# Hybrid mLSTM and attention encoder step: mLSTM heads computed token-major, rotary swap by DVE shuffle, attention heads handled in pairs, on one core

## The reference, cut to what matters

```python
w = jnp.exp(d - m_t[..., None]) * jnp.einsum('bhtd,bhsd->bhts', q, k)
inter = jnp.exp(g - m_t)
num = inter[..., None] * jnp.einsum('bhtd,bhde->bhte', q, C) + jnp.einsum('bhts,bhse->bhte', w, v)
den = inter * jnp.einsum('bhtd,bhd->bht', q, n) + jnp.sum(w, axis=-1)
h = num / jnp.maximum(jnp.abs(den), jnp.exp(-m_t))[..., None]
...
h = h * lax.rsqrt(jnp.mean(h * h, axis=-1, keepdims=True) + EPS)
...
m = jnp.maximum(jnp.max(s, axis=-1, keepdims=True), sk)
p = jnp.exp(s - m)
return p / (jnp.sum(p, axis=-1, keepdims=True) + jnp.exp(sk - m))
```

## Time and profile before

| | us |
|---|---|
| median of 3 runs | 1113.93 (1113.78 to 1116.93) |
| the profiled execution | 1115.43 |
| its span | 1113.6 |
| TensorE busy | 1103.8 (99%) |
| TensorE weight load busy | 1080.8 (97%) |
| DVE busy | 703.9 (63%) |
| ACT busy | 511.2 (46%) |
| POOL busy | 114.1 (10%) |
| mean granted clock, share of full speed | 0.995 |

### The profile page before, as it was taken

The page is one execution under the profiler, slowest core; times in us unless marked ns, Lnnn a source line. Parts: engine busy times, 40 slices in busy tenths (PEclk is TensorE's granted clock), DMA queues, the critical chain, the costliest instruction groups (busy, mean ns, idle before and its releaser), DMA issues.

```text
span 1113.6 us, 21313 instructions
## 1 busy us (share of the span) xinstructions
PE 1103.8 (99%) x8147; PEld 1080.8 (97%) x8147; DVE 703.9 (63%) x1079; ACT 511.2 (46%) x760; POOL 114.1 (10%) x146
## 2 busy tenths in 40 slices
PE   9999999999999999999999999999999999999998
PEld 8999999998999999999999999999988899999998
DVE  7766665474665876665546666655599776666442
ACT  6544443363554544444335444433466554444331
POOL 0000001200002600000210000011142410000011
PEclk9999999999999999999999999999999999999999
DMA  7544454333233644445434445543332244444431
GB/s 274 190 151 173 179 183 178 118 114 109 100 129 111 207 172 167 172 165 206 159 113 168 172 151 173 201 164 142 114 148 92 83 173 160 172 167 179 176 136 43
DMA packets 24493, 172.07 MB, mean 155 GB/s; under 512 B 3280, under 2 KB 3568, under 8 KB 5888
## 3 DMA queue, kind: packets, MB, share of 16 engines
q1 hardware_dynamic: 22320, 167.45, 42.0%
q0 software_dynamic: 960, 2.23, 0.6%
q10 hardware_dynamic: 1168, 1.77, 0.5%
HBM read 168.88 MB, written 2.56 MB: 154 GB/s over the span
## 4 chain that ended last, share of the span: by engine, by line
PE 93%; DVE 4%; ACT 1%; DMA 1%; issue 1%; POOL 0%; SPq 0%; DVEq 0%; ACTq 0%
PE acc L395 30%; PE acc L397 29%; PE acc L396 29%; DVE wlo L382 1%; DMA raw<-in_w 1%; PE num L464 1%; DVE rstd L1042 1%; PE mb L675 0%; PE mb L694 0%; PE mb L609 0%; PE num L601 0%; PE acc L722 0%; ACT work L955 0%; ACT whi L353 0%; PE mb L422 0%
## 5 line engine op out<-in xcount | busy, mean ns | idle before, releaser
L395 PE MATMUL acc<-xhi,whi 128*128 128x288 f32 x1680 | 502.2, 299 | 0.3 <-DVE wlo L382 0.3
L353 ACT ACTIVATE whi<-raw 128x1024 fp32r<-128x1024 f32 (+1 forms) x290 | 326.6, 1128 | 381.2 <-PE acc L397 363.3
L396 PE MATMUL acc<-xlo,whi 128*128 128x288 f32 x1680 | 497.0, 296 | 0.0
L397 PE MATMUL acc<-xhi,wlo 128*128 128x288 f32 x1680 | 495.3, 295 | 0.0
L382 DVE TENSOR_TENSOR wlo<-raw,whi 128x1024 fp32r<-128x1024 f32 (+1 forms) x290 | 384.2, 1326 | 158.0 <-ACT whi L353 147.3
L395 PEld LDWEIGHTS acc<-xhi,whi 128*128 128x128 f32 x1680 | 316.1, 188 | 3.0 <-issue 1.8
L397 PEld LDWEIGHTS acc<-xhi,wlo 128*128 128x128 f32 x1680 | 317.7, 189 | 0.0
L396 PEld LDWEIGHTS acc<-xlo,whi 128*128 128x128 f32 x1680 | 316.8, 189 | 0.5
L395 PE MATMUL acc<-ahi,whi 128*128 128x288 f32 x832 | 247.1, 297 | 0.9 <-DVE alo L1279 0.7
L396 PE MATMUL acc<-alo,whi 128*128 128x288 f32 x832 | 245.4, 295 | 0.0
L397 PE MATMUL acc<-ahi,wlo 128*128 128x288 f32 x832 | 244.6, 294 | 0.0
(11 more groups left out here) (225 smaller groups left out, 642.9 us busy)
## 6 DMA issues: line engine op xcount, KB each, us to landing
raw<-in_w SPq DMA_DIRECT2D x113, 1024.0 KB, 4.8
raw<-in_w SPq DMA_DIRECT2D x32, 1408.0 KB, 5.8
x<-in_xT SPq DMA_DIRECT2D x4, 288.0 KB, 5.3
raw<-in_w SPq DMA_DIRECT2D x4, 256.0 KB, 4.8
out_yT<-x ACTq DMA_DIRECT2D x2, 288.0 KB, 2.2
out_yT<-x SPq DMA_DIRECT2D x2, 288.0 KB, 2.3
work<-in_cst POOLq DMA_DIRECT2D x1, 560.0 KB, 4.2
work<-in_c ACTq DMA_DIRECT2D x1, 514.0 KB
```

The source lines that it names most:

```text
L353: act.activation(dst, src, ACT.Copy).then_inc(hi_done, 1)
L395: pe.matmul(out, wh, hi[:, k, :], start=(first and n == 0), stop=False)
L396: pe.matmul(out, wh, lo[:, k, :], start=False, stop=False)
L397: mm = pe.matmul(out, wl, hi[:, k, :], start=False, stop=(last and n == len(tiles) - 1))
```

## The change

**mLSTM.** The heads' output is now made with tokens on partitions (token-major): for the three token tiles `M_TOK` (0, 128, 160; the last one overlaps, and its last 32 rows are the sample), five matmuls of 257 columns with the weights `wts` as the stationary operand give numerator and denominator together (`vtok` and `c0` have the ones column and the normaliser as 257th). The sum of squares is then ACT's `accum_out`, and denominator, root and scale are columns of 128 x 3, all three tiles at once. DVE scales the heads (`hs`), TensorE transposes them back (6 transposes, step 2), and step 2 also gates them. Steps are four instead of five, at pieces 8, 12, 17 and 22. The gate weights' hi and lo lie side by side in one tile `gw`, so that 16 matmuls do what 24 did. The rows of decays are no longer spread by matmuls: SP writes them to DRAM (`bounce`) and loads them back over all partitions (`through_memory`), behind the load of the stage's sixth unit; six transposes of 4 rows (`row_turn`) give the columns.

**Attention.** Features of a head are laid out so that the swap stays within 32 partitions; DVE's `stream_shuffle` does it, and the ten matmuls of L722 go. POOL multiplies the swapped tile by the sine, DVE the other by the cosine. The items become *pairs*: DVE and ACT do maximum, negation, exps and division of both heads together; one of the pair's scalings goes to ACT (`scaled`). The pair's scores follow a piece (even tick), the values are put into the middle of the next piece (odd tick), and each tick transposes one head. Pieces 4 to 11 carry the pairs 0 to 7. In the tail, more of the partial output products stand between the ticks. The 36 matmuls at the program's end (`long`), whose result nothing reads, are removed.

The core of the diff:

```diff
-SWA_PIECES = ["k0", "q0", "v0", "q1", "q2", "q3", "k1", "q4", "q5", "q6", "v1", "q7"]
+SWA_PIECES = ["k0", "q0", "q1", "v0", "q2", "q3", "k1", "q4", "q5", "q6", "v1", "q7"]
...
+PAIRS = [("p", 0), ("p", 1), ("p", 2), ("p", 3), ("s", 0), ("p", 4), ("p", 5), ("p", 6), ("s", 1), ("p", 7)]
+NP = len(PAIRS)
+PAIR_AT = {4 + n: n for n in range(8)}
+TAIL_TICKS = range(2 * len(PAIR_AT) - 1, 2 * NP + 5)
+
+
+FILL = {16: [(0, [0, 1]), (0, [2, 3]), (1, [0, 1])], 17: [(1, [2, 3])], 18: [(2, [0, 1])],
+        19: [(2, [2, 3]), (3, [0, 1])], 21: [(3, [2, 3])], 23: [(0, [4, 5, 6])], 24: [(m, [4, 5, 6]) for m in (1, 2, 3)]}
+
+HEAD_START = (8, 12, 17, 22)
+HEAD_STEPS = {p + s: (h, s) for h, p in enumerate(HEAD_START) for s in range(4)}
...
+            def through_memory():
+
+                sp.wait_ge(em_ready, 1)
+                sp.dma_start(bounce, r_all).then_inc(bounce_in, 16)
+                sp.wait_ge(bounce_in, 16)
+                every = bounce.rearrange("(a h) n -> a h n", a=1).to_broadcast([P, NH, T + TS])
+                sp.dma_start(spread[:, :, :], every).then_inc(spread_in, 16)
...
+            def row_turn():
+
+                pe.wait_ge(em_ready, 2)
+                for t, at in enumerate(M_TOK):
+                    for q, src in enumerate((r_em, row[0])):
+                        to = (2 * t + q) * NH
+                        mm = pe.transpose(mb[1][:, to:to + NH], src[:, at:at + P], ident[0:NH, 0:NH])
+                mm.then_inc(at_mm, 1)
...
+                    pe.wait_ge(wts_ready, 3 * (h + 1))
+                    N = DV + 1
+                    pe.matmul(mb[0][:, 0:N], wts[:, 0:128], vtok[:, 0, :], start=True, stop=True).then_inc(out_mm, 1)
+                    pe.matmul(mb[1][:, 0:N], wts[:, 128:256], vtok[:, 0, :], start=True, stop=False)
+                    pe.matmul(mb[1][:, 0:N], wts[:, 256:384], vtok[:, 1, :], start=False, stop=True).then_inc(out_mm, 1)
+                    pe.matmul(mb[2][:, 0:N], wts[:, 384:512], vtok[:, 2, :], start=True, stop=False)
+                    pe.matmul(mb[2][:, 0:N], qi[:, :], c0[:, h, :], start=False, stop=True).then_inc(out_mm, 1)
...
-                    pe.wait_ge(den_used, h + 1)
-                    pe.wait_ge(sqs_ready, h + 1)
-                    pe.matmul(mb[2][:, 0:T], ones, sqn[:, 0, :], start=True, stop=True).then_inc(ssq_mm, 1)
+                    pe.wait_ge(hs_ready, 3 * (h + 1))
+                    for t in range(3):
+                        for e in range(2):
+                            mm = pe.transpose(mb[e][:, t * P:(t + 1) * P], hs[:, t, e * P:(e + 1) * P], ident)
+                    mm.then_inc(ht_mm, 1)
...
+            def transposes(n):
+
+                if not 0 <= n < 2 * NP:
+                    return
+                pe.wait_ge(p_ready, n + 1)
+                if PAIRS[n // 2][0] == "p":
+                    pe.wait_ge(p_act, sum(k == "p" for k, _ in PAIRS[:n // 2 + 1]))
+                if n >= 1:
+                    pe.wait_ge(pt_ready, n)
...
+            def values(n, G0):
+
+                if not 0 <= n < NP:
+                    return
+                kind, c = PAIRS[n]
+                pe.wait_ge(pt_ready, 2 * n + 2)
+                pe.wait_ge(evac, G0 + group_of("last", f"v{c // 4 if kind == 'p' else c}") + 1)
+                if n >= 1:
+                    pe.wait_ge(olo_ready, n)
...
+                transposes(t - 3)
+                if t % 2 == 0:
+                    pair_scores(t // 2)
+                else:
+                    values((t - 5) // 2, G0)
...
-                            in_piece(i, 0, c0_ + n, g, G0 + g)
-                    elif what == "swap":
-
-                        pe.wait_ge(evac, max(G0 + group_of("piece", p) + 1, G0 + g - 3))
-                        pe.matmul(bank, perm, s_raw[:, ROPE.index(p) % 2, :], start=True, stop=True).then_inc(turn_mm, 1)
-                    else:
-                        pe.wait_ge(evac, max(G0 + group_of("piece", p) + 1, G0 + g - 3))
-                        for t, (at, m) in enumerate(TOK):
+                            t = 2 * PAIR_AT[n - 1] + 1 if n - 1 in PAIR_AT else None
+                            in_piece(i, 0, c0_ + n, g, G0 + g, between=None if t is None else lambda: tick(t, G0))
+                        if n in PAIR_AT:
+                            tick(2 * PAIR_AT[n], G0)
...
-            long = ahi[:, 0:2, :].rearrange("p a t -> p (a t)")
-            for cols, n in ((P, T), (P, 512), (P, 256), (P, 320), (96, T), (P, P)):
-                for r in range(6):
-                    pe.matmul(acc[2 + r % 2][0:cols, 0:n], whi[:, 0, r, 0:cols], long[:, 0:n], start=True, stop=True)
...
+                    act.activation(warm[:, 7:8], epst[:, :], ACT.Sqrt)
+                    for t in range(3):
+                        act.wait_ge(out_mm, 3 * h + t + 1)
+                        act.activation(hs[:, t, :], mb[t][:, 0:DV], ACT.Square, accum_out=ss[:, t:t + 1]).then_inc(sumsq, 1)
+                    act.wait_ge(y_ready, h + 1)
+                    act.activation(rinv[:, :], dd[:, :], ACT.Sqrt, scale=1.0 / DV).then_inc(sd_ready, 1)
...
+                probs_turned(t - 3)
+                if t % 2 == 0:
+                    scaled(t // 2 - 1)
+                    outputs_hi((t - 6) // 2)
+                    exps(t // 2)
...
+                for n, p in enumerate(SWA_PIECES):
+                    hi_ahead(0, c0_ + n)
+                    if n in PAIR_AT:
+                        if n - 1 in PAIR_AT:
+                            tick(2 * PAIR_AT[n] - 1)
+                        tick(2 * PAIR_AT[n])
...
+                    dve.wait_ge(sumsq, 3 * (h + 1))
+                    den = num[:, :, DV]
+                    own(dve.tensor_copy(dd[:, :], den))
+                    own(dve.tensor_tensor(dd[:, :], dd[:, :], dd[:, :], ALU.mult))
+                    dve.wait_ge(cols_ready, 1)
+                    own(dve.tensor_tensor(dd[:, :], dd[:, :], cols[:, :, 0, h], ALU.max))
+                    dve.scalar_tensor_tensor(dd[:, :], dd[:, :], DV * EPS, ss[:, :], ALU.mult, ALU.add).then_inc(y_ready, 1)
+                    dve.wait_ge(sd_ready, h + 1)
+                    own(dve.reciprocal(rinv[:, :], rinv[:, :]))
+                    for t in range(3):
+                        dve.tensor_scalar(hs[:, t, :], mb[t][:, 0:DV], rinv[:, t:t + 1], None, ALU.mult).then_inc(hs_ready, 1)
...
+                            dve.stream_shuffle(s_sw[:, xi % 2, :], bank, SWAP_16)
+                            dve.tensor_tensor(s_t1[:, xi % 2, :], bank, rc, ALU.mult).then_inc(evac, 1)
+                        if n in PAIR_AT:
+                            scores(PAIR_AT[n])
+                        lo_ahead(0, c0_ + n)
+                        if n in PAIR_AT:
+                            outputs_lo(PAIR_AT[n] - 3)
+                            divide(PAIR_AT[n])
...
```

More of the change, by code:

```diff
@@ new lines, in exps @@
+            def exps(n):
+                if n >= NP:
+                    return
+                b = n % 2
+                parts = ((0, P), (P, 3 * P)) if PAIRS[n][0] == "p" else ((0, CACHE + TS),)
+                act.wait_ge(neg_ready, n + 1)
+                for u in range(2):
+                    for j, (lo_, hi_) in enumerate(parts):
+                        v = prob[:, (2 * n + u) % 4, lo_:hi_]
+                        act.activation(v, v, ACT.Exp, bias=s_neg[:, b, u, j:j + 1], accum_out=s_sum[:, b, u, j:j + 1])
+                act.wait_ge(z_exp, n + 1)
+                J = len(parts)
+                act.activation(s_sk[:, b, :, 0:J], s_z[:, b, :, 0:J], ACT.Exp).then_inc(exp_ready, 1)
@@ new lines, in divide @@
+            def divide(n):
+                if not 0 <= n < NP:
+                    return
+                b = n % 2
+                p = PAIRS[n][0] == "p"
+                parts = ((0, P), (P, 3 * P)) if p else ((0, CACHE + TS),)
+                J = len(parts)
+                dve.wait_ge(exp_ready, n + 1)
+                own(dve.tensor_tensor(s_den[:, b, :, 0:J], s_sum[:, b, :, 0:J], s_sk[:, b, :, 0:J], ALU.add))
+                dve.reciprocal(s_inv[:, b, :, 0:J], s_den[:, b, :, 0:J]).then_inc(inv_ready, 1)
+                dve.wait_ge(inv_ready, n + 1)
+                for u in range(2):
```

651 lines of the change are left out of this document (287 added, 364 removed).

## The result

| | before | after |
|---|---|---|
| median, us | 1115.43 (1113.78 to 1118.40, 4 runs) | 1127.17 (1125.98 to 1129.44, 4 runs) |
| the profiled execution | 1115.43 | 1125.98 |
| its span | 1113.6 | 1124.2 |
| ratio of after to before | | 1.011, 95% interval 1.0093 to 1.0127 |
| TensorE busy | 1103.8 | 1084.5 |

The kernel became 1.1% slower, by 11.7 us, where 5.4 were forecast; 1127.17 lies 0.2 us above the range. TensorE has 19 us less of busy time, and the kernel is slower all the same: the work went and waits came. The medians leave out a single execution, one of the twelve of run 1, which took 1461.53 us at a mean granted clock of 0.675.

What follows compares the result with a forecast made beforehand. TensorE's work was taken as the price, with any new wait added whole. mLSTM -10.4 and attention +15.8 us summed to +5.4: 1120.8 us profiled, 1119.3 us median (0.5% slower), with an 8-in-10 range of 1105 to 1127.

Steps and rivals of the forecast that it cites:

- mLSTM heads, TensorE work: mLSTM stage: rebuilt steps save TensorE 1.9 us for each of four heads, -7.6 us.
- row spreads and their two clock drops: mLSTM: transposes replace the 4-row spreading matmuls, -4.8 us, and two stretches at low clock go, -3.0 us.
- waits for the scaled heads: mLSTM: TensorE waits before step 2, 0.3 us three times and 3.7 us at the last head, together +4.6 us.
- clock behind them: mLSTM: one drop of TensorE's clock after the idle time at the last head, +1.5 us.
- slots of pieces 5 and 6: Attention's first two slots: nothing to transpose at their ends, so 4.6 and 4.8 us.
- slots of pieces 8 to 11: Attention: four slots of 8.84, 7.8, 8.75 and 8.8 us, both waits in the order of queues included.
- tail: From piece 11's end to the end of the partial output products: 30.3 us against 25.50, +4.8 us.
- The two waits in the slots: Attention slots: TensorE idles 1.74 us for ACT's copy behind its split, 1.16 us for DVE's outputs_lo; slot 8.84 us.
- One clock drop after the 3.7: +1.5: Attention, slot of piece 7: TensorE waits 3.7 us for ACT, then one low-clock stretch costs 1.5 us.
- the clock falls in the slots too: Rival: repeated waits in attention slots lower TensorE's clock, six drops of 1.5 us, 1128 us; chance 0.12.
- the slots keep TensorE's pace: Rival: in attention ACT's copy and DVE's outputs_lo come in time, slots take 5.7 us, 1097 us in all; chance 0.16.
- Only the first wait: Rival: DVE's scores and split end 1.2 us sooner, slots and tail 6 us shorter, 1113 us; chance 0.22.

Runs made afterwards that it cites:

- run 1: Changed kernel with ACT's copy of the head transposed in mid-piece put ahead of its split of weights: 1115.36 us, ratio 1.0001 to the kernel before.
- run 2: Changed kernel with DVE's outputs_lo put ahead of its split of weights, behind the scores: 1123.05 us, ratio 1.0069 to the kernel before.
- run 3: Changed kernel with both the edits of run 1 and run 2: 1111.08 us, ratio 0.9955 to the kernel before.
- run 4: Changed kernel with 29 unread products of zeros filling TensorE's wait in the slot of piece 7: 1124.11 us, ratio 1.0075 to the kernel before.
- run 8: Kernel of run 3 with the partial output products behind piece 11 moved and reordered: 1105.81 us, ratio 0.9908 to the kernel before.
- run 9: Changed kernel with the edits of run 3, run 6, run 7 and run 8 together: 1097.48 us, ratio 0.9850 to the kernel before.
- run 5: The mLSTM part of the change alone, attention and its projection as in the kernel before: 1101.96 us, ratio 0.9879 to the kernel before.
- run 7: Kernel of run 3 with ACT's copy of the very first transposed head ahead of the second pair's exps: 1107.21 us, ratio 0.9924 to the kernel before.
- run 6: Changed kernel with the last mLSTM head's step 2 behind two pieces of partial output products: 1121.05 us, ratio 1.0050 to the kernel before.
- run 10: Kernel of run 5 with the last mLSTM head's step 2 behind two pieces of partial products: 1097.76 us, ratio 0.9852 to the kernel before.

## Why the prediction was right and wrong

The direction and the two places in the queues were right; the size was half of what was measured, since the low clock in attention was put at 1.5 us and cost about 5, and the time fell just outside the range. Two errors partly cancelled: mLSTM gave 2.1 us more than forecast, and attention with what follows it cost 7.5 us more. Without the first the miss would have been larger. By the steps of the sum, profiled execution against profiled execution (measured: from the times at which the pieces' last products start, and the waits as the trace has them):

| step | forecast | measured |
|---|---|---|
| mLSTM heads, TensorE work | -7.6 | -8.6 |
| gates | -1.1 | -1.1 |
| row spreads and their two clock drops | -7.8 | -7.8 |
| waits for the scaled heads | +4.6 | +3.3 |
| clock behind them | +1.5 | +1.6 |
| attention to piece 4 | -1.1 | -1.3 |
| slots of pieces 5 and 6 | 4.6 and 4.8 | 5.84 and 4.56 |
| slot of piece 7, clock in it | 9.8 + 1.5 | 12.79 |
| slots of pieces 8 to 11 | 34.2 | 34.75 |
| tail | 30.3 | 32.92 |
| rest of the projection, and the block behind | 0 | +1.6 and +0.4 |

**mLSTM: right.** -12.5 against -10.4. The row spreads, the gates and the trip through memory (no wait, as taken) came out to a tenth of a microsecond. Heads 0 to 2 had none of the 0.3 us waits, and the last waited 3.31 us instead of 3.7. For the matmul of 32 rows the forecast took the price of its row. TensorE: Matmul & The Clock Gate of the Trainium skill (table "Why this matters for your kernels") has a K=32 matmul as long as one of K=128. The traces here speak for the row: with 257 columns one of 32 rows took 0.63 us before, and one of 128 rows 0.43 from start to start after. The heads gave 8.6 us, where the row's price made it 7.6 and the equal price 6.8; no run changed the rows alone.

**The two waits in the slots: right, in place, releaser and length.** Forecast 1.74 and 1.16 us, measured 1.68 and, in the slots of pieces 8 and 10, 1.17 and 1.28 (0.54 and 0.89 in the other two); a slot 8.84, measured 9.00. Runs 1 to 3 take them away one by one.

**The step that failed: the size of the clock drops in attention.** "One clock drop after the 3.7: +1.5" took 3.41 us at the low level from the opening. The wait was there (3.93 us), and 6.82 us at 0.50 came behind it; run 4 prices them at 2.8 us. For the tail no drop was in the sum at all, and one of 6.83 us came; no run took it away alone, but two profiles price such a stretch. Runs 8 and 9 have the same instructions from the end of piece 11 to the end of the projection; run 8 has 3.41 us at 0.50 there and takes 40.24 us, run 9 has none:

```profile
834.72:873.70 38.98, 36.49 (x295) 32.66 (x294) 26.94 (x72) 22.94 (x58) 16.75 (x18) 1.00 0.28 92
```

That is 1.3 us for 3.41, so about 2.5 for 6.83, an estimate; the tail was 2.6 above forecast. So where the sum had 1.5 us for the clock in attention, the runs show some 5. The price of one stretch of 3.41 us, 1.5 in the sum, was if anything too high; how long the low clock would last and in how many places it would come was what the sum had too small. I had held these for one rival, "the clock falls in the slots too", with its price in six slots and a chance of 0.12. What came lay between: not in every slot, but in two places, each twice as long as the 3.41 us of the row. That middle belonged in the forecast's own range.

**What was overlooked.** The first scores wait 1.25 us for POOL's rotation (L1480), which is the whole excess of the slot of piece 5; before, 0.35 us of idle time stood at that place. And the projection's fifth piece waits 1.4 us for its split, since the first four pieces all end within 12 products of each other; I looked at the tail up to its last partial product and at nothing behind it. Run 8 takes that wait away.

**Profile and median.** The sum gave 1120.8 for a profiled run and I took 1.5 off for the median, since the profiled run of before stood above that of three. The new profiled run stood 1.2 below its median instead. So of the 7.9 us between forecast and median 2.7 are only the choice of runs, and the range should have had room for them. The profiled execution is the fastest of the four of the changed kernel. The two slowest (1128.00 and 1129.44 us) have mean clocks of 0.983 and 0.982 against its 0.988, so they spent more time at the low clock than the rows here show.

The rivals: "the slots keep TensorE's pace" is what run 3 shows for pieces 8 to 11 once both waits are gone (5.9 us, forecast 5.7), but even with everything mended attention gained nothing; its remaining waits stand mostly in the slots of pieces 5, 7 and 8, which that rival left out. "Only the first wait" is out, as the changed kernel had both.

## What to carry to other kernels

Where a change joins small steps into larger ones, ask of each result that another engine waits for what its engine does first: here a copy of 0.47 us stood behind a split of 1.06 that nobody needed for four pieces, and a 0.42 us subtraction behind one of 1.22. Two swaps of lines were worth 16 us, more than the whole mLSTM part gave; such a place is seen in the order of the queues, and its length is read from rows of before. Time the parts of a change alone: half of this one gave 13.4 us and the other half took that back and 11.7 more.

## What the runs showed of the hardware

- **The low clock behind a wait isn't a fixed price.** TensorE waited 3.3 us for the last mLSTM head in eight of these kernels. Behind it 0.50, the 1.2 GHz level, lasted 3.4 us in five of the profiles, 6.8 us in one (run 8) and did not come in two (runs 5 and 7). Without the wait (runs 6, 9 and 10) it did not come. What decides this stays open, but it isn't the kernel alone, since executions of one kernel differ. Of 37 executions of the kernel before, taken beside the experiments, four have a mean clock of 1.000 and took 1112.3 to 1112.8 us; twenty have 0.994 or 0.995, which is what the profile with its three stretches of 3.41 us has, and took 1114.9 to 1118.4. The means lie 3.7 us apart, 1.2 for a stretch if there were three. So the two drops behind the row spreads, priced at 3.0 in the sum, were not in every execution either.
- **It moves.** In pieces 8 to 11 TensorE waited up to 1.7 us at a time in the changed kernel and in runs 2, 4 and 6, and up to 1.3 in run 1. In the profiles of the changed kernel and of runs 1 and 6 the clock there was 1.00; in those of runs 2 and 4 it had a mean of 0.90, though run 2 has fewer waits there than the changed kernel. One profile for each kernel can't tell a habit of the kernel from chance.
- **A wait that is removed can be worth more than its length.** By its trace run 1 has 8.3 us less of waits in attention than the changed kernel (15.5 instead of 23.8), and gave 11.8 in the median and 10.6 from profile to profile: its two low stretches there were 3.4 us long each instead of 6.8, which at 1.3 us for 3.41 comes to about 2.5.
- **POOL's rotation took twice its usual time beside DVE's split of weights.** This is most of the 1.25 us for which the first scores waited. POOL's third and fourth multiplication of 288 columns at the start of attention, a later one, and DVE's split at the same time:

```profile
795.51 0.81 POOL L1477 TENSOR_TENSOR work<-work 128x288 f32<-128x288 f32 x1
796.40 1.66 POOL L1480 TENSOR_TENSOR work<-work 128x288 f32<-128x288 f32 x1
...
799.17 0.80 POOL L1477 TENSOR_TENSOR work<-work 128x288 f32<-128x288 f32 x1
```
```profile
796.16 1.25 DVE L392 TENSOR_TENSOR wlo<-raw,whi 128x1024 fp32r<-128x1024 f32 x1
```

Of the 20 such multiplications in the changed kernel's profile four lie beside a split for over 1 us, and these took 1.66 to 1.81 us; the other 16, beside a split for 0.2 us at most, took 0.79 to 0.81, also where DVE was busy with the shuffle. Time beside a split isn't the whole rule: in run 1 one of them lay beside a split for 0.76 us and took 0.81. No run moved the split away from the rotation.
